# Attention step of a two-layer mixer: the items beside the scores issued ahead of the next step's scores, on TensorE and ScalarE

## What is computed

```python
def block_attention(q, k, v):
    # 8 query heads, 2 key/value heads, head size 64, blocks of 128 queries
    s = jnp.einsum('bqkgd,bskd->bkgqs', qblk, k, preferred_element_type=jnp.float32) * scale
    p = jax.nn.softmax(s, axis=-1).astype(v.dtype)
    return jnp.einsum('bkgqs,bskd->bqkgd', p, v)

# latent tokens: queries attend to all latent keys and the 128 cached context keys
k_all = jnp.concatenate([apply_rope(k, cos, sin), ctx_k.astype(k.dtype)], axis=1)
o_attn = block_attention(q_r, k_all, v_all)
```

## Time and profile before

| | us |
|---|---|
| median of 3 runs | 1811.63 (1811.22 to 1812.18) |
| time of the profiled execution | 1813.14 |
| its span in the profile | 1811.5 |
| TensorE busy in it | 1672.2 (92%) |
| VectorE busy | 1005.5 (56%) |
| GpSimd busy | 931.0 (51%) |
| ScalarE busy | 621.9 (34%) |

### The profile page before, as it was taken

How to read it: one execution, slowest core, us unless ns; L and a number is a source line. 1 busy time by engine, 2 the same in 40 slices (tenths; PEclk the granted TensorE clock), 3 DMA queues, 4 the chain that set the end, 5 groups by cost and what they waited for, 6 DMA issues and landing times. The chain is left out here.

```text
span 1811.5 us, 40795 instructions
## 1 busy us (share of the span) xinstructions
PE 1672.2 (92%) x17412; PEld 1360.8 (75%) x17412; DVE 1005.5 (56%) x1476; ACT 621.9 (34%) x1238; POOL 931.0 (51%) x856
## 2 busy tenths in 40 slices
PE   4999999979988999999849999999799889999998
PEld 2898999969986555558628989999699765555586
DVE  2655316457845877792126553064578467777821
ACT  4312310134443444461133223101344434445601
POOL 1003396069953978853210033960799539788522
PEclk9899999989999999999969999999899999999999
DMA  9211112210000001132283111122100000010322
GB/s 338 97 45 60 62 56 63 88 44 22 5 9 16 7 20 32 31 123 93 93 308 121 33 60 62 59 66 82 44 22 4 12 13 7 26 31 27 123 101 85
DMA packets 71246, 117.22 MB, mean 65 GB/s; under 512 B 10128, under 2 KB 42128, under 8 KB 71056
## 3 DMA queue, kind: packets, MB, share of 16 engines
q1 hardware_dynamic: 70128, 114.18, 18.6%
q10 hardware_dynamic: 928, 0.34, 0.1%
HBM read 95.03 MB, written 19.47 MB: 63 GB/s over the span
## 5 line engine op out<-in xcount | busy, mean ns | idle before, releaser
L1432 POOL TENSOR_TENSOR attn_accp<-attn_accp,attn_pr 128x1024 f32<-128x1024 f32 x110 | 269.4, 2449 | 42.3 <-ACT attn_pr L1498 36.6
L93 PE MATMUL ps<-h_hi,in_w_hi 128*128 128x384 f32 (+1 forms) x816 | 275.6, 338 | 5.1 <-DVE h_lo L456 4.9
L94 PE MATMUL ps<-h_lo,in_w_hi 128*128 128x384 f32 (+1 forms) x816 | 273.9, 336 | 0.0
L95 PE MATMUL ps<-h_hi,in_w_lo 128*128 128x384 f32 (+1 forms) x816 | 273.8, 336 | 0.0
L1701 DVE TENSOR_REDUCE attn_ql<-ps 128x1 f32<-128x1152 f32 x128 | 173.0, 1355 | 108.2 <-PE ps L1619 108.0
L1498 ACT ACTIVATE attn_pr<-ps 128x512 f32<-128x512 f32 x292 | 158.6, 595 | 170.8 <-PE ps L1663 162.0
L93 PEld LDWEIGHTS ps<-h_hi,in_w_hi 128*128 128x128 f32 (+1 forms) x816 | 149.7, 183 | 14.2 <-issue 6.7
L94 PEld LDWEIGHTS ps<-h_lo,in_w_hi 128*128 128x128 f32 (+1 forms) x816 | 149.6, 183 | 3.9
L95 PEld LDWEIGHTS ps<-h_hi,in_w_lo 128*128 128x128 f32 (+1 forms) x816 | 149.5, 183 | 3.9
L1662 PEld LDWEIGHTS ps<-attn_QH,attn_KH 128*128 128x128 f32 x292 | 55.0, 188 | 124.9 <-ACT attn_pr L1498 55.2
L1672 PE MATMUL ps<-attn_pr,z 128*64 128x512 f32 x520 | 139.5, 615 | 0.0
(11 more groups left out here) (252 smaller groups left out, 3660.5 us busy)
## 6 DMA issues: line engine op xcount, KB each, us to landing
in_w<-in_w_in SPq DMA_DIRECT2D x22, 1024.0 KB, 6.0
zz<-in_w_mod SPq DMA_DIRECT2D x8, 2048.0 KB, 13.4
gates<-in_gate SPq DMA_DIRECT2D x48, 192.0 KB, 1.9
z<-out_y SPq DMA_DIRECT2D x18, 512.0 KB, 4.4
attn_gt<-gates SPq DMA_DIRECT2D x34, 256.0 KB, 2.6
z<-in_x_sample SPq DMA_DIRECT2D x16, 512.0 KB, 5.1
z<-in_w_mod SPq DMA_DIRECT2D x4, 2048.0 KB, 10.1
out_w<-in_w_out SPq DMA_DIRECT2D x16, 512.0 KB, 6.0
```

The source lines that it names most:

```text
L93: nc.tensor.matmul(out, a_hi(i), b_hi(i), start=(i == 0), stop=False)
L94: nc.tensor.matmul(out, a_hi(i), b_lo(i), start=False, stop=False)
L95: last = nc.tensor.matmul(out, a_lo(i), b_hi(i), start=False, stop=(i == n - 1))
L1432: nc.gpsimd.tensor_tensor(acc, a, pr[:, n % 4], ALU.add).then_inc(pool_added, 1)
```

## The change

In both loops the step's items move ahead of the next step's scores or exponentials. Nothing is added or removed, and no other engine's program changes.

```diff
@@ scalar
         exponentials(0)
         for n, items in enumerate(steps):
+            for item in items:
+                evict(item)
             if n + 1 < len(ATTN_STEPS):
                 exponentials(n + 1)
-            for item in items:
-                evict(item)
@@ tensor
         scores(0)
         work(first[-1])
         for n, items in enumerate(steps):
+            for item in items:
+                work(item)
             if n + 1 < len(ATTN_STEPS):
                 scores(n + 1)
-            for item in items:
-                work(item)
             weighted_values(n)
```

## The result

| | before | changed |
|---|---|---|
| median, us | 1811.58 (1806.82 to 1813.21, 11 runs) | 1820.09 (1814.21 to 1826.88, 11 runs) |
| ratio of the two, 95% interval | | 1.0052 (1.0038 to 1.0067) |
| profiled execution (span) | 1813.14 (1811.5) | 1822.88 (1821.2) |

What follows compares the result with a forecast made beforehand. TensorE was taken to set the pace in attention, with GpSimd close behind early on. Terms gave +2.7 us a layer, +5.1 with 0.85 for clock and 1.5 for collisions; two layers, +10.2 on 1811.6, made 1822, range 1815 to 1831.

Steps and rivals of the forecast that it cites:

- a pause with clock and some collisions: The forecast itself: TensorE's pause in step 7, a clock fall and some VectorE collisions, 1818 to 1831 us; chance 0.58.
- (e): VectorE operations meeting GpSimd adds: step 28's wait goes, -0.78; uncertain collisions in steps 9, 13, 27, +1.5 us a layer.
- (a): Start of attention: step 0's maximum fits into TensorE's wait ahead of the second scores, -0.52 us a layer.
- (b): Six sums a layer lose their neighbouring values of 64-column weights: +0.35 us each, +2.1 a layer.
- (c): Step 7: TensorE's turn of pair 3 waits for GpSimd's late split, 3.3 us instead of 1.1, +2.2 a layer.
- (d): Behind step 7's pause TensorE's clock may halve: 1.7 us where it falls, counted as 0.85 a layer.
- the row at 363: Earlier pause in the profile: TensorE busy 0.67 of 3 us, then granted 0.51 of its clock for 7 us.
- that at 795: Like pause in layer 1: TensorE busy 0.88 of 3 us, at no cost in clock.
- Faster emptying: Rival: ten waits of o come from exponentials ahead of the emptying, up to 8.5 us go, about 1805; chance 0.06.
- GpSimd's chain not holding: Rival: GpSimd does not hold TensorE longer; only sums, start and step 28 count, 1813.2 us, no change; chance 0.10.
- Neither clock nor collisions: Rival: no clock fall and no VectorE collisions, +2.7 us a layer, 1817 us; chance 0.19.
- All collisions and 7 us of half clock: Rival: every collision falls wrong and the clock halves for 7 us each layer, up to 1835; chance above 1831, 0.07.

Runs made afterwards that it cites:

- e9: Kernel before with the new order in step 0 only, on TensorE and ScalarE: 1811.06 us, ratio 0.9985.
- e1: Changed kernel, but a sum that ends its step goes back behind the next scores, its emptying behind the exponentials: 1813.6 us, ratio 1.0004.
- e2: Changed kernel, but GpSimd splits pair 3 ahead of its power instead of behind it and two adds: 1822.29 us, ratio 1.0046.
- e5: Changed kernel with pair 3 split ahead of the power and the DeltaNet items (oscale and o) four steps later: 1813.59 us, ratio 0.9997.
- e4: Changed kernel, but steps 1 to 8 in the order of before on TensorE and ScalarE: 1814.77 us, ratio 1.0003.
- e7: Kernel before, order unchanged, with pair 3 split ahead of the power and oscale and o four steps later: 1807.07 us, ratio 0.9964.
- e3: Kernel before with GpSimd's split of pair 3 ahead of the power: 1813.57 us, ratio 0.9997.
- e6: Changed kernel with the early split, oscale and o four steps later, and sums back behind the next scores: 1809.21 us, ratio 0.9966.
- e8: Kernel before with ScalarE's new order alone, emptying before its exponentials, TensorE in the old order: 1839.69 us, ratio 1.0154.
- e10: Kernel before with the early split, oscale and o four steps later, and step 0 alone in the new order: 1808.57 us, ratio 0.9983.

## Why the prediction was right, point by point

**The forecast** was 1822 within 1815 to 1831, slower; measured 1820.09. Of the likeliest case, a pause with clock and some collisions, the pause and the clock came. The collisions did not, and the number is as near as it is by luck: see (e) and the sum below it.

**(a) The start**, -0.52: right. The maximum stands ahead of the scores (581.57), and e9 shows the gain alone, 0.51.

**(b) Sums**, +0.35 each, a step of 3.87: right. 3.85 to 3.88 measured, 0.36 a sum by e1. Two layers of six sums are 4 of the 8.5 us. The steps around a sum give a little back: from the scores of step 39 to those of step 48, nine steps with one sum, the changed kernel takes 26.38 us and the kernel before 26.11, so 0.27 more and not 0.35. The prediction has 0.1 a layer for hidden loads; this is 0.08 in every nine steps, by estimate some 0.5 over the layer.

**(c) The wait for GpSimd**, 1.1 to 3.3 with the turn at 605.7: right in time and size. The turn came at 606.60, with attention starting 0.9 later (579.27 against 578.36), so 605.7 on the scale of before; the power began 1.7 later (593.91 against 592.20), of which 0.8 is the chain's own delay, as worked out. The pause is 3.4. What it missed is who holds TensorE in its first part. The prediction named one holder; the trace shows 1.5 of the 3.4 behind a blocked `oscale`. The split still sets the pause's end (606.45, the turn at 606.60), so the size came out right. But power, adds and split are one chain on GpSimd, and the maximum hangs on it by way of VectorE as the turn does by way of the split. Had I proposed the early split as a cure, as I did in e2's expectation, it would have failed.

**(d) Clock**, 1.7 where it falls: right in layer 1. Against the earlier trace rows, values take 1.88 by starts instead of 1.01 (608.11 to 609.99) and the maximum with its switch 1.13 instead of 0.62: 1.4 of loss in two groups, with the rest of the 4 us window at 0.57 some 1.5. It fell in both layers, where I had counted a half chance each, so the 0.85 a layer in the sum was too little by some 0.65; the row at 363 was the nearer one, not that at 795. The Trainium skill (TensorE: Matmul & The Clock Gate, What's actually happening) ties the half rate to idling, and the pause of step 7 agrees with it: 0.57 and 0.50 behind it, 1.00 in e5 where it is gone. Layer 2's start is not told apart by idling: 6.8 us at half there in the changed kernel, e4 and e7, 3.4 us in e1, and 1.00 in before, e2, e3, e5, e6, e8, e9 and e10 (in e9 it was layer 1's start that had 3.4 us), although in all of these TensorE waits the same 1.8 us for VectorE just ahead of the first scores. Since e7 has the old order, this fall is not bound to the change. What decides it stays open; it is worth 2.7 us of the profiled execution, and how often it came in the timed runs is not known.

**(e) Phase of VectorE**: wrong for the collisions, +1.5 a layer in the sum where the measured cost is nothing. The wait of step 28 went, as predicted (675.46 starts without one), and the gates of 36, 45 and 54 escaped. The three collisions called uncertain (steps 9, 13, 27) cost TensorE nothing; at step 9 the `oscale` did meet an add (609.27, 2.58 us), while TensorE was at half clock. The one that held TensorE is the `oscale` of step 7, inside the pause of (c), where it costs nothing of its own.

By this account layer 1 is -0.52 (start) + 6 x 0.32 (sums) + 2.3 (pause, 3.4 instead of 1.1) + 1.5 (clock) - 0.26 (step 3, 0.25 of wait instead of 0.51) - 0.78 (step 28) - 0.07 = +4.1, against 3.6 measured; the 0.5 between them is the size of what the steps around the sums give back (b). In the prediction's own sum the -0.17 is nowhere named; only the -0.07 of step 16 can be found in it. The forecast of +5.1 a layer was too high by the collisions' 1.5, and too low by 0.65 for the clock. In the profiled execution layer 2's start, which the prediction did not have, added 2.7, and so the two layers came to 9.9 where 10.2 was forecast. That agreement is luck; the mechanisms of (a) to (d) are not.

**The rivals.** Faster emptying: wrong, the waits of `o` are 0.7 as before, and e8, ScalarE's part alone, loses 15 us a layer. GpSimd's chain not holding: wrong by the 1.74 at 606.60. Neither clock nor collisions: wrong about the clock, and right that no collision outside the pause held TensorE. All collisions and 7 us of half clock: wrong in both, the fall of step 7 was 3.4 us in each layer.

## What to carry to other kernels

In a steady chain on one engine, putting a step's items ahead of the next step's main work is the same cycle cut elsewhere. What counts are its ends, which groups of like weights it parts, and the one place where a slow chain of another engine crosses it. Before a stall is charged to the operation that its bracket names, look for a second one on the same chain, and ask what the cure puts ahead of it: splitting early gained nothing here, since it delayed the power by 1.6 us, while splitting early with the outputs moved out of the power's way gained 3.5 us a layer. And run the control: the same two moves on the kernel before were worth 1.7 us a layer, more than the new order ever gave.

## What the runs showed of the hardware

- **Parting two 64-column groups** costs 0.32 to 0.36 us each time. Side by side the two take 1.86 us and apart 2.02, which is 0.16; the rest, by estimate from rows 3, is about 0.10 each for going into and out of one more such group.
- **VectorE beside GpSimd.** An `oscale` of 128x256, both inputs in SBUF, took 2.61, 2.57 and 2.60 us when it began with an add of GpSimd, and 0.41 where it stood alone. The Trainium skill (GPSIMD Engine Reference, Key points) says that the two share an interface for such instructions; the rows agree, and show that VectorE's instruction ends only behind GpSimd's. The reads from PSUM kept their 1.34 to 1.36.
- **The clock fell after a smaller pause than I had thought.** In e1, TensorE was busy 1.53 of 3 us, with one wait of 1.47, before the clock stood at 0.66 over the next 5 us, while 0.88 of 3 at 795 had cost none. A row of busy share does not settle beforehand whether it falls.
